# Sparse attention: projections reordered, the whole convolution on TensorE in column tiles, compression in column tiles

## What is computed

```python
h = rms_norm(x, attn_norm_g[layer])
proj = einsum('bsd,de->bse', h, w_in[layer])          # 2328 columns
q, k_c, v_c, k_s, v_s, k_w, v_w, g_logit, u = split(proj)
q = rope(rms_norm(q));  k_slc, k_win likewise         # 8 query heads, 2 key heads, 64 wide
k_cmp, v_cmp = compress_blocks(k_c), compress_blocks(v_c)   # 15 blocks of 32 tokens, gelu(blocks @ w1) @ w2
attn_out = gated sum of attention over compressed, selected, window keys
a, g = split(u)                                       # 512 + 512, the gated unit
y = causal depthwise conv, 31 taps, of a * sigmoid(g) # 512 channels
conv_out = silu(layer_norm(y))
x = x + concat(attn_out, conv_out) @ w_out[layer]
```

## Time and profile before

| | us |
|---|---|
| median of 3 executions | 2441.9 (2441.86 to 2445.96) |
| profiled execution, its own time | 2442.8 |
| its span, first to last instruction | 2441.1 |
| TensorE busy | 2401.8 |
| VectorE busy | 1770.4 |
| ScalarE busy | 1465.7 |
| mean granted TensorE clock | 0.994 of full |

### The profile page before, as it was taken

One profiled execution on the slowest core, in us unless ns is written; L12 is line 12 of the kernel. 1 busy time (PEld: TensorE's weight loads), 2 busy tenths in 40 slices (PEclk: granted clock), 3 DMA queues, 4 the chain that ended last, 5 costly groups with the idle time before them and its releaser, 6 DMA issues.

```text
span 2441.1 us, 31541 instructions
## 1 busy us (share of the span) xinstructions
PE 2401.8 (98%) x11768; PEld 1997.6 (82%) x11768; DVE 1770.4 (73%) x2230; ACT 1465.7 (60%) x1822; POOL 103.6 (4%) x115
## 2 busy tenths in 40 slices
PE   9999999999999999999999999999999999999998
PEld 8888888887888888888888888888878888887886
DVE  7964446778988989898989898857465565755554
ACT  7544445556777777777777777665544445554443
POOL 1400000400100000000000000001000000000000
PEclk9989999999999999999999999999999999999999
DMA  8225554405999999999999999724535542453551
GB/s 305 75 90 202 182 194 147 171 19 209 357 350 372 346 370 348 367 350 366 348 370 350 367 352 372 244 77 173 190 109 190 184 148 94 156 190 104 190 190 43
DMA packets 244951, 565.30 MB, mean 232 GB/s; under 512 B 9136, under 2 KB 15728, under 8 KB 244848
## 3 DMA queue, kind: packets, MB, share of 16 engines
q1 hardware_dynamic: 244848, 563.90, 65.3%
HBM read 562.82 MB, written 1.05 MB: 231 GB/s over the span
## 4 chain that ended last, share of the span: by engine, by line
PE 86%; issue 8%; DVE 3%; ACT 3%; DMA 0%; SPq 0%; POOL 0%; DVEq 0%; POOLq 0%; ACTq 0%
PE PS L886 24%; PE PS L888 24%; PE PS L887 24%; PE PS L1074 3%; PE PS L1039 2%; PE PS L1051 1%; ACT SM L1717 1%; PE PS L958 1%; PE PS L1416 1%; PE PS L1300 1%; DVE HTl L2120 1%; PE PS L1261 1%; PE PS L1425 1%; PE PS L983 1%; PE PS L1441 1%
## 5 line engine op out<-in xcount | busy, mean ns | idle before, releaser
L2519 DVE TENSOR_TENSOR Wl<-ring,Wh 128x2048 fp32r<-128x2048 f32 x334 | 761.6, 2298 | 101.1 <-ACT Wh L1854 101.0
L1854 ACT ACTIVATE Wh<-ring 128x2048 fp32r<-128x2048 f32 x334 | 639.9, 1919 | 127.6 <-PE PS L888 127.6
L2113 DVE TENSOR_TENSOR Wl<-ring,Wh 128x2048 fp32r<-128x2048 f32 (+2 forms) x192 | 430.6, 2251 | 281.9 <-ACT Wh L1624 281.7
L1624 ACT ACTIVATE Wh<-ring 128x2048 fp32r<-128x2048 f32 (+2 forms) x192 | 361.2, 1890 | 221.4 <-PE PS L888 220.3
L886 PE MATMUL PS<-Wh,HTh 128*128 128x512 f32 (+3 forms) x1184 | 465.3, 393 | 3.8 <-DVE Wl L2113 3.5
L888 PE MATMUL PS<-Wh,HTl 128*128 128x512 f32 (+3 forms) x1184 | 457.5, 386 | 0.0
L887 PE MATMUL PS<-Wl,HTh 128*128 128x512 f32 (+3 forms) x1184 | 456.6, 386 | 0.0
L886 PE MATMUL PS<-Wh,xgh 128*128 128x512 f32 x896 | 354.6, 396 | 1.8 <-DVE Wl L2519 1.2
L888 PE MATMUL PS<-Wh,xgl 128*128 128x512 f32 x896 | 349.8, 390 | 0.0
L887 PE MATMUL PS<-Wl,xgh 128*128 128x512 f32 x896 | 349.2, 390 | 0.0
L886 PEld LDWEIGHTS PS<-Wh,HTh 128*128 128x128 f32 x1184 | 223.6, 189 | 48.4 <-DVE Wl L2113 3.8
(11 more groups left out here) (334 smaller groups left out, 2628.4 us busy)
## 6 DMA issues: line engine op xcount, KB each, us to landing
ring<-in_moe_w_gate SPq DMA_DIRECT2D x112, 1024.0 KB, 7.1
ring<-in_moe_w_up SPq DMA_DIRECT2D x112, 1024.0 KB, 7.4
ring<-in_moe_w_down SPq DMA_DIRECT2D x112, 1024.0 KB, 6.9
ring<-in_mlp_w SPq DMA_DIRECT2D x64, 1024.0 KB, 5.1
ring<-in_w_in SPq DMA_DIRECT2D x27, 1024.0 KB, 5.2
ring<-in_w_out SPq DMA_DIRECT2D x16, 1024.0 KB, 6.3
ring<-in_cross_wkv SPq DMA_DIRECT2D x16, 1024.0 KB, 12.0
ring<-in_ffn_w_gate SPq DMA_DIRECT2D x14, 1024.0 KB, 5.1
```

The costliest lines, as they stand in the source:

```text
L1624: act.activation(Wh[:, i % SPLITS, 0:n], ring[:, r % RING, 0:n], ACT.Copy).then_inc(w_hi, 1)
L1854: act.activation(Wh[:, (base + i) % SPLITS, :], ring[:, (raw + i) % RING, :], ACT.Copy).then_inc(e_hi, 1)
L2113: dve.tensor_tensor(Wl[:, i % SPLITS, 0:n], ring[:, r % RING, 0:n], Wh[:, i % SPLITS, 0:n].bitcast(F32), ALU.subtract).then_inc(w_lo, 1)
L2519: dve.tensor_tensor(Wl[:, (base + i) % SPLITS, :], ring[:, (raw + i) % RING, :], Wh[:, (base + i) % SPLITS, :].bitcast(F32), ALU.subtract) ...
```

## The change

What it does:

- The projection blocks come in the order queries, keys with compression inputs, window keys and gates, then the gate half of the gated unit. The fifth block (the other half, `GLU_A0`) is done by halves and tiles, with the compression, the transposes of queries and keys, the position product and the first scores between its quarters. The multiplication by the sigmoid is done by VectorE straight from PSUM (`glu`).
- The gated unit is transposed as `extras` behind unit 0 of attention. SP then copies each chunk of `CT` into a ring slot by four DMAs of 32 channels, each channel four times, shifted by 0 to 3 tokens (`shifted`).
- Conv: a product contracts over 32 channels x 4 shifts and gives 32 output partitions; 8 quads of taps x 4 groups of 32 channels make a chunk, 32 products with 128x32 weights. The four groups write four ranges of 32 partitions of one PSUM bank. The eight half chunks stand at the places of `CONV_SLICES`; VectorE adds the bias (`CONV_OUT`). No tap is left on VectorE.
- Weights: once, in layer 0, `tap_selection` spreads the taps over partitions by 32 small products behind the first tile of the second block; VectorE makes its 0/1 operands (`selections`) and copies the result. Per layer GpSimd builds four weight tiles (`conv_weights`), after the last projection product, in the memory of `HTh`.
- Compression: 32 products on four column ranges in turn, eight steps, one position product instead of two.
- On VectorE the first split of layer 0 stands ahead of the squares; the head norms are done for queries and for keys apart.

```diff
-PE_TAPS = 28
+ROWS = 32
+GROUPS = P // ROWS
+SHIFTS = P // ROWS
+QUADS = (TAPS + SHIFTS - 1) // SHIFTS
+SHIFTED = S + SHIFTS * (QUADS - 1)
+CT_W = SHIFTED + SHIFTS
 UNREAD = 3
-LIN1 = 21
-FAR = CC - 2
-FAR_TAPS = 20
-CONV_OPS = [(j, ch) for j in range(TAPS) for ch in range(FAR + (j >= FAR_TAPS))] + [(j, CC - 1) for j in range(PE_TAPS, TAPS)]
+LIN1 = 19
+CONV_SLICES = {(2, 2): (0, 0), (3, 0): (0, 1), (4, 1): (1, 0), (5, 0): (1, 1), (6, 1): (2, 0), (7, 0): (2, 1), (8, 1): (3, 0), (8, 2): (3, 1)}
+CONV_OUT = {4: 0, 6: 1, 8: 2, 9: 3}
...
-        far_w = nc.alloc_sbuf_tensor_at("far_w", [P, TAPS, P], F32, offset=ht_at)
+        conv_w = nc.alloc_sbuf_tensor_at("conv_w", [P, CC, GROUPS * QUADS, ROWS], F32, offset=ht_at)
...
-        IN1_BLOCKS = [(GLU_A0, 512), (GLU_G0, 512), (0, 512), (512, 512), (1024, 280)]
+        IN1_BLOCKS = [(0, 512), (512, 512), (1024, 280), (GLU_G0, 512), (GLU_A0, 512)]
...
+        def shifted(layer, ch):
+
+            return ring[:, (conv_raw[layer] + ch) % RING, 0:GROUPS * SHIFTED].rearrange("p (j s) -> p j s", j=GROUPS)
...
-                for i, name in enumerate(("cmp_w1_k", "cmp_w1_v")):
+                for name in ("cmp_w1_k", "cmp_w1_v"):
                     w1 = a[name][layer].rearrange("(l p) h -> p l h", p=P)
-                    plain(w1, CMP_STRIDE, CMP_HID, i + 2)
-                c.lin += 1 + 3 + 3
-                for n in range(2):
-                    lin_block(a["w_out"][layer], n * 512, 512)
+                    plain(w1, CMP_STRIDE, CMP_HID, 1)
+                c.lin += 1
+                lin_block(w, *IN1_BLOCKS[4])
+                c.lin += 1 + 3
+                lin_block(a["w_out"][layer], 0, 512)
+                _, turns_at, c.pt = pt_order(nsa_units(), nsa_extras, c.pt)
+                for ch in range(CC):
+                    r = len(users)
+                    sp.wait_ge(*users[r - RING])
+                    sp.wait_ge(pt_out, turns_at[ch // 2] + 1)
+                    for j in range(GROUPS):
+                        src = CT[ROWS * j:ROWS * (j + 1), ch, :]
+                        windows = bass.AP(src.tensor, src.offset, [src.ap[0], [1, SHIFTS], [1, SHIFTED]])
+                        sp.dma_start(shifted(layer, ch)[:, j, :], windows).then_inc(
+                            shift_ld[ch] if j < GROUPS - 1 else w_ld[r % RING], 16)
+                    users.append((conv_full, layer * CC + ch + 1))
+                lin_block(a["w_out"][layer], 512, 512)
...
+            def conv_weights(layer, chunks):
+
+                for ch in chunks:
+                    taps = tap_rows[:, layer, ch].rearrange("p j q -> p (j q)")
+                    pool.tensor_tensor(conv_w[:, ch, :, :], taps.unsqueeze(2).to_broadcast([P, GROUPS * QUADS, ROWS]),
+                                       row_mask[:].unsqueeze(1).to_broadcast([P, GROUPS * QUADS, ROWS]),
+                                       ALU.mult).then_inc(conv_w_ok, 1)
...
-            pool.wait_ge(cols_ld, 16)
...
+                power(T * HEADS, T * 2 * KV_HEADS)
+                pool.wait_ge(taps_out, 1)
+                pool.wait_ge(lin_full, layer * LIN1 + 11)
+                conv_weights(layer, (0, 1))
+                power(2)
+                conv_weights(layer, (2, 3))
+                power(T)
...
+            def tap_selection():
+
+                pe.wait_ge(sel_ok, 1)
+                taps = cols[:, 0:LAYERS * C1W].rearrange("p (l c) -> p l c", l=LAYERS)[:, :, C1["cw"]:C1["cw"] + CC * TAPS]
+                taps = taps.rearrange("p l (c j) -> p l c j", j=TAPS)
+                for j in range(GROUPS):
+                    into = PS[:, j, 0:LAYERS * CC * QUADS].rearrange("p (l c q) -> p l c q", l=LAYERS, c=CC)
+                    rows_ = slice(ROWS * j, ROWS * (j + 1))
+                    for l in range(LAYERS):
+                        for s_ in range(SHIFTS):
+                            mine = taps[rows_, l, :, s_::SHIFTS]
+                            mm = pe.matmul(into[:, l, :, 0:mine.shape[-1]], spread[rows_, s_, :], mine, start=(s_ == 0),
+                                           stop=(s_ == SHIFTS - 1))
+                mm.then_inc(taps_full, 1)
...
+                k_rows = c.lin + 2
+                linear(IN1_BLOCKS[1][1], after_tile=tap_selection if layer == 0 else None)
+                linear(IN1_BLOCKS[2][1])
+                linear(IN1_BLOCKS[3][1], after_tile=lambda: (added(k_rows), pe.wait_ge(taps_out, 1), turn(t_cmp)))
...
+                def compress(bank):
+
                     pe.wait_ge(blk_ready, layer + 1)
                     pe.wait_ge(sel_ok, 1)
-                    w = plain(CMP_STRIDE, CMP_HID)
-                    for l in range(CMP_STRIDE):
-                        mm = pe.matmul(PS[0:2 * NCMP + 1, bank, 0:CMP_HID], kblk[:, v, l, :], w[:, l, :],
-                                       start=(l == 0), stop=(l == CMP_STRIDE - 1))
+                    w = []
+                    for v in range(2):
+                        r = cmp_raw[layer] + v
+                        pe.wait_ge(w_ld[r % RING], 16 * (r // RING + 1))
+                        w.append(raw_slot(r, CMP_STRIDE, CMP_HID))
+                    steps = CMP_STRIDE // 2
+                    for step in range(steps):
+                        for tile in range(4):
+                            v, l = tile // 2, tile % 2 * steps + step
+                            mm = pe.matmul(PS[CMP_COLS * tile:CMP_COLS * (tile + 1), bank, 0:CMP_HID], kblk[:, v, l, :],
+                                           w[v][:, l, :], start=(step == 0), stop=(step == steps - 1))
...
+                def conv(ch, part):
+
+                    if part == 0:
+                        r = conv_raw[layer] + ch
+                        pe.wait_ge(conv_w_ok, layer * CC + ch + 1)
+                        pe.wait_ge(shift_ld[ch], 16 * (GROUPS - 1) * (layer + 1))
+                        pe.wait_ge(w_ld[r % RING], 16 * (r // RING + 1))
+                        if layer * CC + ch:
+                            pe.wait_ge(conv_out, layer * CC + ch)
+                    moving = shifted(layer, ch)
+                    for q in range(part * QUADS // 2, (part + 1) * QUADS // 2):
+                        for j in range(GROUPS):
+                            mm = pe.matmul(PS[ROWS * j:ROWS * (j + 1), 6, 0:S], conv_w[:, ch, j * QUADS + q, :],
+                                           moving[:, j, SHIFTS * q:SHIFTS * q + S], start=(q == 0), stop=(q == QUADS - 1))
+                    if part == 1:
+                        mm.then_inc(conv_full, 1)
...
+                w = split_slot(piece(), HALF, n)
+                half_products(0, 0, w)
+                compress(cmp_bank)
+                half_products(0, 1, w).then_inc(w_half, 1)
+                rows()
+                turn(t_nsa)
+                w = split_slot(piece(), HALF, n)
+                kc_bank = lin_bank()
+                added(cmp_lin)
+                pe.matmul(PS[:, kc_bank, 256:316], hid_rows_sb, with_pos[:].rearrange("p v n -> p (v n)"), start=True,
+                          stop=True).then_inc(turned, 1)
+                c.turn += 1
+                half_products(1, 0, w).then_inc(lin_full, 1)
                 begin()
+                half_products(1, 1, w).then_inc(lin_full, 1)
                 if layer == 0:
...
-                finish(rows)
+                finish({4: rows})
...
+                act.activation(hid[:, 0, 0:8], ident[:, 0:8], ACT.Gelu_apprx_tanh)
+                c.piece += 1
+                ahead()
+                take(hid_rows_sb)
+                c.piece += 1
+                ahead()
                 turn(t_nsa)
+                c.lin += 2
                 act.wait_ge(turned, c.turn + 1)
                 act.activation(hid[:].rearrange("p v n -> p (v n)"), PS[:, 4 + c.lin % 4, 256:316],
                                ACT.Gelu_apprx_tanh).then_inc(turn_out, 1)
                 c.turn += 1
+                act.activation(rs[:, 40:48], ident[:, 0:8], ACT.Exp)
...
+            def selections():
+
+                folded = norm_tmp[:, 0:CMP_COLS]
+                dve.memset(with_pos[:], 0.0)
+                dve.memset(spread, 0.0)
+                dve.tensor_reduce(row_mask[:], ident[:].rearrange("p (c s) -> p c s", s=SHIFTS), AX, ALU.add)
+                seq(dve.tensor_reduce(folded, ident[:].rearrange("p (j n) -> p n j", n=CMP_COLS), AX, ALU.add))
+                for v in range(2):
+                    half = slice(64 * v, 64 * v + 64)
+                    dve.tensor_tensor(with_pos[half, v, :], folded[half, 0:2 * NCMP],
+                                      folded[half, 2 * NCMP:2 * NCMP + 1].to_broadcast([64, 2 * NCMP]), ALU.add)
+                for s_ in range(SHIFTS):
+                    ins = dve.tensor_copy(spread[:, s_, :].rearrange("p (c s) -> p c s", s=SHIFTS)[:, :, s_], folded)
+                ins.then_inc(sel_ok, 1)
...
-                    dve.wait_ge(cols_ld, 16)
+                    c.piece += 1
+                    ahead()
...
```

(19 more changed lines are left out.)

312 lines of the change are left out of this document (132 added, 180 removed).

## The result

The change made the kernel slower: 2461.27 us (median of 4, 2459.92 to 2464.44) against 2441.89 (4 runs, 2441.86 to 2445.96), ratio 1.0081, 95% interval 1.0069 to 1.0093. The forecast was 2441.0, no difference that can be told. The profiled execution took 2464.4 us with a span of 2462.6; before it was 2442.8 and 2441.1, so the two traces differ by 21.5 us, 2 more than the medians.

What follows compares the result with a forecast made beforehand. TensorE, busy 98% of the span, was taken as the bound. Two layers at -6.85 us give -13.7, layer 0's once-only work +12.8, total -0.9: 2441.0 us for the median; range 2428 to 2469, the forecast's own 2436 to 2446.

Steps and rivals of the forecast that it cites:

- once-only term: Layer 0: selection, its wait and a slow clock stretch, less a wait that goes; +12.8 us in sum.
- the two layers: Per layer: work removed -28.15, conv +13.9, array switches +1.6, compression +3.7, waits +2.1; -6.85 us, two layers -13.7.
- rival 4: Clock falls longer, in the selection itself or at the thin start of attention: +7, 2448 us; chance 0.14.
- Conv in column groups: Conv per layer: 256 passes, four column groups abreast, 13.9 us, plus 1.6 for eight switches of the array's shape.
- rivals 1 and 2: Conv and compression: column groups don't overlap, 2531 us, chance 0.13; or three or two abreast, 2450 or 2469, chance 0.13.
- rule weighed: Conv: products start and end in program order, so neighbours could overlap only pairwise and the conv would take 27.7 us.
- Compression: Per layer: 64 passes in column groups, 3.5 us and 0.2 for the switch, 3.7 us; bounds 1.8 and 7.1.
- Waits in attention: Per layer: TensorE's waits for compression result, second transpose, first conv slice and bias additions; 5.0 us instead of 2.9.
- wait for the selection matrices: Layer 0, behind the second block's first tile: TensorE waits for VectorE's matrices, 3.5 us; bounds 2 and 6.
- selection, 64 passes: Layer 0: 32 products, thin passes one after another at 0.11 us each, 7.0 us; 1.8 if row groups ran abreast.
- products behind it at the lower level (38.9 to 44.4): Layer 0: one slow clock stretch of 6.8 us costs half its length, 3.4 us; bounds 0 and 10.4.
- rival 3: Layer 0's selection is cheap, row groups overlapping (1.8 us) and no clock fall: +4.2 instead of 12.8, 2432.4 us; chance 0.28.

Runs made afterwards that it cites:

- e4: The kernel after the change with the passes of one column group in a row, then the next group's, in conv and compression: 2516.94 us, ratio 1.0301.
- e10: e9 with the bias additions of the first three channel groups one iteration earlier in VectorE's order: 2437.69 us, ratio 0.9981.
- e14: e10 with only the first conv slice moved behind the scores and probabilities of iteration 3: 2431.18 us, ratio 0.9957.
- e1: The kernel after the change with ScalarE's sine and exponential one projection block earlier, and VectorE's lambdas right behind the angles: 2453.48 us, ratio 1.0051.
- e2: The kernel after the change with 8 of the 32 tap selection products, shifts 1 to 3 left out: 2445.46 us, ratio 1.0015.
- e5: The kernel after the change without tap selection on TensorE; eight small transfers and masked VectorE products instead: 2450.23 us, ratio 1.0033.
- e6: The edits of e5 and e1 together, on the kernel after the change: 2450.58 us, ratio 1.0037.
- e11: e10 with the fifth block's first split ahead of the norms, taps after the last splits, first conv slice one turn later: 2435.30 us, ratio 0.9969.
- e13: The kernel after the change with the four row groups of the tap selection taking turns: 2450.98 us, ratio 1.0044.
- e3: The kernel after the change with the tap selection one block later and VectorE taking its result behind the query norms: 2457.25 us, ratio 1.0052.
- e9: e5 with layer 0's splits ahead of angles and norms, sine and exponential after the third block, taps loaded later: 2440.74 us, ratio 0.9992.
- e12: The kernel after the change, selection still on TensorE, with only e9's orders of VectorE and ScalarE: 2460.80 us, ratio 1.0076.
- e7: The kernel before the change with only the compression in four column groups and one product after it instead of two: 2447.12 us, ratio 1.0024.
- e8: e6 with six unread products instead of three in each of iterations 10 to 12 of sparse attention: 2453.61 us, ratio 1.0049.

## Why the prediction was wrong

The forecast for the trace was -0.9 us and the trace shows +21.5. The 22.4 between them are 12.4 in the once-only term (forecast +12.8, measured 25.2), 10.8 in the two layers (forecast -6.85 each, measured -1.47 in layer 1), and 0.8 that came back elsewhere. The time lies inside the wide range, 2428 to 2469, but by luck: its upper end was the price of column groups two abreast, which did not happen. The signs of rival 4 did come, a clock at 0.50 between 28 and 46 us and more of it at the start of attention, but its price was +7.

**Conv in column groups: right.** Forecast 13.9 + 1.6 us a layer for 256 passes four abreast; measured 8 x 1.93 = 15.4. The row of the scores, two row groups abreast, carried over to four column groups, and rivals 1 and 2 are refuted. What the forecast didn't see is the condition: e4 shows 143 ns a pass when eight of a group stand in a row. The 27.7 of the rule weighed rested on an inference of the prediction, that neighbours overlap only pairwise. The Trainium skill (TensorE: Matmul & The Clock Gate, Part 3) itself says that products start and end in program order; the records of a slice don't name their product, so no run here shows whether they do. The traces refute the pairwise limit: passes start in fours. Against a pass of 217 ns by itself four alternating groups are 3.6 times as fast, edges included, more than the 2.38 for three that the Trainium skill gives in the same part.

**Compression: too dear.** 3.7 forecast, 1.95 measured: four abreast here too, 1.75 a layer better; it is nearly all by which the first stretch of layer 1 beat the forecast (-20.75; the forecast's terms there sum to about -19).

**Waits in attention: too small.** 5.0 forecast a layer. Measured in layer 1 are 0.46 ahead of the first probabilities (0.4 forecast), 6.07 in the middle stretch and 0.87 ahead of the channel mean behind it, 7.4 together. The first conv slice waited 2.36 (1.8 forecast), the second transpose 1.35 (1.6); the bias additions cost 2.0 and the 0.87 (1.2). The forecast charged mask and addition against the transposes of the same iteration. It left out that VectorE's queue ahead of them holds the end of the unit before, which waits for its values: ahead of the seventh slice VectorE ends that wait at 524.49, is through with the maxima at 526.19 and adds at 526.27, and TensorE goes on at 526.89. e10 and e14 took most of it out, and layer 1 became 8.1 us faster than before: the forecast's -6.85 was there to be had, not in this order.

**End of attention: no term.** Work unchanged, +4.0 us in layer 1, because 14 of 25 us ran at the lower level instead of 5 of 21. Layer 0 is the same: its last stretch grew from 22.80 to 27.07 us, with 20.5 us at the lower level. This part differs between traces of kernels whose code is the same there: in layer 0, e1, e2, e5, e6, e11, e13 and e14 show 3.4 + 6.8 us, e3, e9, e10 and e12 20.5, and e3 and e9 20.5 in layer 1 too. Within one kernel the time goes with the mean clock: e7's executions go from 2441.7 us at 0.992 to 2454.9 at 0.985. Each kernel has one trace, so it isn't shown that this part makes the difference between executions. What decides it is open; denser products (e8) didn't pay. It also stands in the medians: e1, e2 and e13 lie 0.6 to 4.2 us further under after than the table behind e14 says, and their traces lack the long stretch that after's has.

**Once in layer 0: the step that failed.** Forecast +12.8, measured +25.2 (the 23.7 lost up to layer 1, and the 1.5 that a layer by itself gains). The terms:

| term | forecast | measured |
|---|---|---|
| wait for the selection matrices | 3.5 | 2.92 |
| selection, 64 passes | 7.0 | 11.37 |
| products behind it at the lower level (38.9 to 44.4) | 3.4 | 2.6 |
| gap ahead of the gate's block | 0 | 4.90 |
| products behind that gap at the lower level (to 64.9) | 0 | 1.8 |
| lower level at the start of attention (2 x 3.4 us), less a shorter conv wait | 0 | 2.9 |
| wait ahead of the output projection | 0 | 1.85 |
| gap of before that goes | -1.06 | -1.06 |

Products at the lower level take 427 instead of 227 ns, so such a stretch loses 47% of its length. The terms up to the compression (all but the 2.9 and the 1.85) sum to 22.5; the first stretch of layer 0 grew by 1.68 us where layer 1's shrank by 20.75, 22.4 apart. The 2.9 fit too: the middle grew by 18.05 against 15.24. The 1.85 is real but no cost of its own, as the last stretch grew by 4.3 us with it and by 4.0 in layer 1 without it; that is why the column sums to 27.3 and not to 25.2. Three faults. First, the selection: rival 3 (row groups abreast, 1.8) and the forecast (one after another at 0.109) were both priced at full clock. The price of a pass was right: in e12, whose first passes ran at the full level, they start 112 ns apart. In after they start 213 ns apart at the lower level (178 on average, with some overlap where groups meet), so it is the clock, rival 4's mechanism, that made 11.37 of it. The order was the other half: e13 shows 2.43 us with alternating groups. Second, the gap of 4.90: the forecast followed TensorE's queue past the selection, but not VectorE's and ScalarE's past the shorter third block. Angles, sine, exponential and the norms of the queries stand in front of the gate's split there; e1 took 7.8 us off by moving two of them. Third, the clock was priced as one new stretch of 6.8 us behind the selection; layer 0 had five stretches, 51 us in all, where before had two of 6.8.

The terms don't simply add. Three quarters of the selection are worth 15.8 us (e2; 11.6 in the first stretch), the sine 7.8 (e1; 7.2), yet without any selection that stretch was only 7.2 us shorter and the kernel 8 us over before (e5), because VectorE's once-only work then stood bare. With that order repaired too (e9) the stretch is 18.3 us shorter, and of the 22.4 about 4.2 are left, the gap ahead of the fifth block. e12 confirms it from the other side: with the selection back in, the stretch is 16.5 us longer, as nothing hides beneath it.

## What to carry to other kernels

Put the row or column group of the array in the innermost loop. Passes on different groups ran fully abreast when they alternated; with eight or sixteen passes of one group in a row they overlapped only where two groups met (60 against 143 ns a pass, 30 against 93). With four in a row nothing was lost that the trace shows (e2, 42 ns). When work is moved on the bound engine, walk the in-order queues of its feeders through the same stretch and put the splits that it waits for ahead of everything that is needed later. A faster step on the bound engine is worth its time only if its feeders are ready by then (e7). A gap followed by thin passes cost twice here: the clock stayed down 17.1 us in after, and 6.8 and 3.4 where the thin passes were fewer (e13, e2). Where the time varies from execution to execution, compare one stretch of the traces beside the medians.

## What the hardware showed that was not expected

- Four column groups of 128x32 weights: 32 passes of 256 columns in 1.93 us (60 ns each), 64 of 128 columns in 1.95 (30 ns). In turn: 4.59 and 5.96 us. Alternating, they start in fours, 216 ns apart at 256 columns.
- Four row groups of 32x128 weights, 32 columns or fewer a pass, sixteen of a group in turn: starts 112 ns apart at the full level (e12) and 213 at the lower (after). Alternating: 38 ns a pass over both levels (e13).
- With gaps of 2.6 to 3.7 us ahead, the lower level lasted 17.1 us where 11.4 us of thin passes in turn came behind the gap (after, e1, e3), 6.8 where it was 2.4 us (e13), 3.4 where it was 0.7 us (e2). Not every such gap did it: at e5's first (2.70 us, dense products on both sides) the clock stayed up.
